# First mixer of a decoder trunk: head squares made in z's place, the inverse's transposed seed by TensorE, q halves emptied as done, scan-only products inside later merges

## What is computed

```python
c_q, c_kv, k_r, qkv, z, b_logit, a_logit = jnp.split(h @ w_in, idx, axis=-1)
q  = (rms_norm(c_q, q_norm) @ w_q_b)           # 8 heads of 96
kv = (rms_norm(c_kv, kv_norm) @ w_kv_b)        # 8 heads of 64 + 64
y_mla = causal_block_attention(rope(rms_norm(q)), rope(rms_norm(k)), v)
gq, gk, gv = jnp.split(silu(causal_short_conv(qkv, conv_w)), 3)   # 8 heads of 64 each
gq, gk = l2_norm(gq) * 64 ** -0.5, l2_norm(gk)                    # per head
# gated delta rule in 4 chunks of 64 tokens, per head:
a    = strict_lower(kb @ k.T * decay) + eye
u, w = triangular_solve(a, [vb, kb * exp(gc)])
attn = (q @ k.T) * decay;  q_dec = q * exp(gc)
for each chunk:                                 # the scan
    v_new = u - w @ state
    o     = q_dec @ state + attn @ v_new
    state = state * exp(g_last) + k_tail.T @ v_new
o = rms_norm(o, out_norm) * silu(z)
y = concat([y_mla, o]) @ w_out
```

## Time and profile before

| | |
|---|---|
| time, median of 3 | 1108.63 us (1105.33 to 1108.97) |
| profiled execution, its time | 1108.93 us |
| its span, first to last instruction | 1107.1 us |
| mean granted clock of TensorE | 0.994 |
| TensorE busy | 98% of the span |
| VectorE, ScalarE, GpSimd busy | 58%, 46%, 4% |

### The profile page before, as it was taken

The page is one execution under the profiler, slowest core; times in us unless marked ns, Lnnn a source line. Parts: engine busy times, 40 slices in busy tenths (PEclk is TensorE's granted clock), DMA queues, the critical chain, the costliest instruction groups (busy, mean ns, idle before and its releaser), DMA issues.

```text
span 1107.1 us, 18807 instructions
## 1 busy us (share of the span) xinstructions
PE 1081.3 (98%) x8329; PEld 987.0 (89%) x8329; DVE 647.3 (58%) x791; ACT 503.8 (46%) x597; POOL 47.1 (4%) x34
## 2 busy tenths in 40 slices
PE   7999999998889999999999999999999999999998
PEld 7999988987789799999889999888788889999986
DVE  5755544688665775555447555544764557555542
ACT  5644433683633354444335444434654536444430
POOL 1000000112051000000000000000100000000000
PEclk9999999999899999999999999999999999999999
DMA  9855555253002356555546565555445474665531
GB/s 311 265 181 187 189 190 178 87 190 114 1 15 68 126 184 189 188 190 191 190 152 194 188 190 191 190 185 176 153 159 218 155 228 154 192 189 190 191 114 38
DMA packets 127194, 184.91 MB, mean 167 GB/s; under 512 B 4205, under 2 KB 101722, under 8 KB 126986
## 3 DMA queue, kind: packets, MB, share of 16 engines
q1 hardware_dynamic: 126368, 181.88, 50.6%
q0 software_dynamic: 448, 1.71, 0.5%
q10 hardware_dynamic: 298, 0.12, 0.1%
HBM read 182.66 MB, written 1.05 MB: 166 GB/s over the span
## 4 chain that ended last, share of the span: by engine, by line
PE 88%; DVE 7%; ACT 2%; issue 2%; DMA 1%; POOLq 0%; SPq 0%; POOL 0%; DVEq 0%; ACTq 0%
PE B L1274 19%; PE B L1275 19%; PE B L1276 19%; PE B L1315 7%; PE B L1319 7%; PE B L1316 7%; PE B L1688 3%; DVE wlo L840 2%; DVE arena L1007 1%; PE B L1384 1%; PE B L1385 1%; PE B L1386 1%; DMA raw<-in_ffn_w_up 1%; PE B L1348 1%; PE B L1811 1%
## 5 line engine op out<-in xcount | busy, mean ns | idle before, releaser
L840 DVE TENSOR_TENSOR wlo<-raw,whi 128x2048 fp32r<-128x2048 f32 (+1 forms) x169 | 387.7, 2301 | 227.5 <-ACT whi L443 227.3
L443 ACT ACTIVATE whi<-raw 128x2048 fp32r<-128x2048 f32 (+1 forms) x171 | 324.2, 1908 | 385.2 <-PE B L1276 243.0
L1274 PE MATMUL B<-xTh,whi 128*128 128x256 f32 x1408 | 397.4, 282 | 0.3 <-DVE wlo L840 0.2
L1275 PE MATMUL B<-xTl,whi 128*128 128x256 f32 x1408 | 396.4, 282 | 0.0
L1276 PE MATMUL B<-xTh,wlo 128*128 128x256 f32 x1408 | 396.4, 282 | 0.0
L1274 PEld LDWEIGHTS B<-xTh,whi 128*128 128x128 f32 x1408 | 266.1, 189 | 1.2 <-DVE wlo L840 0.7
L1275 PEld LDWEIGHTS B<-xTl,whi 128*128 128x128 f32 x1408 | 266.3, 189 | 0.0
L1276 PEld LDWEIGHTS B<-xTh,wlo 128*128 128x128 f32 x1408 | 266.2, 189 | 0.0
L1315 PE MATMUL B<-whi,hTh 128*128 128x512 f32 x352 | 139.5, 396 | 0.0
L1316 PE MATMUL B<-wlo,hTh 128*128 128x512 f32 x352 | 139.0, 395 | 0.0
L1319 PE MATMUL B<-whi,hTl 128*128 128x512 f32 x352 | 110.6, 395 | 0.0
(11 more groups left out here) (241 smaller groups left out, 999.6 us busy)
## 6 DMA issues: line engine op xcount, KB each, us to landing
raw<-in_ffn_w_up SPq DMA_DIRECT2D x44, 1024.0 KB, 5.4
raw<-in_ffn_w_down SPq DMA_DIRECT2D x44, 1024.0 KB, 4.8
raw<-in_ffn_w_gate SPq DMA_DIRECT2D x43, 1024.0 KB, 5.5
raw<-in_sg_w_in SPq DMA_DIRECT2D x16, 1024.0 KB, 5.4
raw<-in_ab_w_in SPq DMA_DIRECT2D x8, 1024.0 KB, 5.1
raw<-in_sg_w_out SPq DMA_DIRECT2D x8, 1024.0 KB, 5.3
raw<-in_ab_w_out SPq DMA_DIRECT2D x4, 1024.0 KB, 4.8
raw<-in_ab_w_in SPq DMA_DIRECT2D x2, 832.0 KB, 4.4
```

The source lines that it names most:

```text
L443: A(whi[:, j % SLOTS, 0:kt * width], raw[:, j % SLOTS, 0:kt * width], ACT.Copy).then_inc(S("hi_ready"), 1)
L840: TT(wlo[:, j % SLOTS, 0:n], raw[:, j % SLOTS, 0:n], whi[:, j % SLOTS, 0:n].bitcast(f32), ALU.subtract).then_inc(S("lo_ready"), 1)
L1274: mm(out_ap, lh, rh, start=first, stop=False)
L1275: mm(out_ap, lh, rl, start=False, stop=False)
```

## The change

Five things, all in the first mixer. The memory places of the squares, of DT and of qd^T change with them.

1. ScalarE empties the q product's first half (t = 0) as soon as that half is done, ahead of `hi(b + 8)`; the semaphore `latent_sums` counts the first halves of q and kv.
2. VectorE makes `lo(b + 10)` right after `conv(3)` instead of after `scale_channels(4)`.
3. The head squares get one buffer, `head_squares`, where z will stand later. ScalarE squares q after `nt_out(1)`, and k after `tap(5)` once VectorE has summed q's. VectorE sums q's between `lo(b + 11)` and `conv(5)`, k's after `conv(5)`. z is copied only after both sums.
4. DT's seed is D's seed transposed by TensorE in heads 6 and 7 of the attention, through bank B3, copied by ScalarE.
5. The gram of q moves into level 2, the transpose of Am into level 3, the transposes of qd into level 4, each between a level's M1 products and its DT M1 products.

```diff
-        k_squares, q_squares = at(XT0 + 2048, 1024), at(XT0 + 3072, 1024)
+        head_squares = at(R0 + 4448, 1024)
@@ ScalarE
-            hi(b + 8)
-            act.wait_ge(S("unit_done"), B_UNIT + 1)
             for t in range(NT):
+                act.wait_ge(*((S("latent_sums"), 1) if t == 0 else (S("unit_done"), B_UNIT + 1)))
                 q0, q1 = (B[6], B[7]) if t == 0 else (B[0], B[1])
...
+                if t == 0:
+                    hi(b + 8)
...
             nt_out(1)
+            act.wait_ge(S("nt_out"), 2)
+            A(head_squares, QKVn[0].rearrange("p t n -> p (t n)"), ACT.Square).then_inc(S("head_squares"), 1)
             tap(3)
...
             tap(5)
+            act.wait_ge(S("nt_out"), 4)
+            act.wait_ge(S("head_sums"), 1)
+            A(head_squares, QKVn[1].rearrange("p t n -> p (t n)"), ACT.Square).then_inc(S("head_squares"), 1)
             for i in range(4):
                 qkT_out(i)
...
             act.wait_ge(S("unit_done"), Z_UNIT + 2)
+            act.wait_ge(S("head_sums"), 2)
             for t in range(NT):
                 A(SZ[:, t, :], B[t][:], ACT.Copy, scale=rstd[:, t:t + 1]).then_inc(S("z_out"), 1)
-            act.wait_ge(S("nt_out"), 4)
-            A(k_squares, QKVn[1].rearrange("p t n -> p (t n)"), ACT.Square).then_inc(S("head_squares"), 1)
-            A(q_squares, QKVn[0].rearrange("p t n -> p (t n)"), ACT.Square).then_inc(S("head_squares"), 1)
...
+                if h >= 6:
+                    t = h - 6
+                    act.wait_ge(S("dt_sums"), t + 1)
+                    A(DT[:, 512 * t:512 * t + 512], B[3][:], ACT.Copy).then_inc(S("dt_ready"), 1)
@@ VectorE
             conv(3)
+            lo(b + 10)
...
             scale_channels(4)
-            lo(b + 10)
             conv(4)
...
+            def head_sums(i):
+                dve.wait_ge(S("head_squares"), i + 1)
+                nc.vector.tensor_reduce(qk_head_ss[:, i, :], head_squares.rearrange("p (m d) -> p m d", d=DK),
+                                        AX.X, ALU.add).then_inc(S("head_sums"), 1)
+
             scale_channels(5)
             lo(b + 11)
+            head_sums(0)
             conv(5)
 
-            for i, a in enumerate((q_squares, k_squares)):
-                dve.wait_ge(S("head_squares"), 2 - i)
-                link(nc.vector.tensor_reduce(qk_head_ss[:, i, :], a.rearrange("p (m d) -> p m d", d=DK), AX.X, ALU.add))
+            head_sums(1)
+            dve.wait_ge(S("head_sums"), 2)
...
-            for t in range(NT):
-                dve.wait_ge(S("lt_ready"), t + 1)
-                link(TT(h3(DT, t), h3(LT, t), eight("level1"), ALU.mult))
-                TT(h3(DT, t), eight("eye64"), h3(DT, t), ALU.subtract).then_inc(S("dt_ready"), 1)
@@ TensorE
+                if h >= 6:
+                    pe.wait_ge(S("d_ready"), h - 5)
+                    if h == 6:
+                        pe.wait_ge(S("dT_out"), 4)
+                    else:
+                        pe.wait_ge(S("dt_ready"), 1)
+                    problems(h - 6, 3, D, None).then_inc(S("dt_sums"), 1)
```

More of the change, by code:

```diff
@@ L227, in build_trunk @@
         Lm, LT, AT = at(R0, 1024), at(3072, 1024), at(R0 + 5472, 1024)
-        D, DT, M1 = at(R0 + 1280, 1024), at(8192, 1024), at(2048, 1024)
+        D, DT, M1 = at(R0 + 1280, 1024), at(XT0 + 2048, 1024), at(2048, 1024)
         kbe, kt = at(9216, 1024), at(10240, 1024)
-        k_squares, q_squares = at(XT0 + 2048, 1024), at(XT0 + 3072, 1024)
-        kT, qT, qdT, wT = [at(XT0 + 1024 * i, PAIRS, SEQ) for i in range(4)]
+        head_squares = at(R0 + 4448, 1024)
+        kT, qT, qdT, wT = [at(o, PAIRS, SEQ) for o in (XT0, XT0 + 1024, 8192, XT0 + 3072)]
         qd = at(1024, NT, 512)
@@ L1125, in _ @@
                     dve.wait_ge(S("decay_exps"), 2)
[L1126 removed]
+                    link(TT(begc, beta, egc, ALU.mult))
                     dve.wait_ge(S("dec_exp"), 1)
@@ L1167, in _ @@
                        ).then_inc(S("m1_ready"), 1)
+                if n == 2:
+                    dve.wait_ge(S("dec_masked"), 1)
+                    for odd in range(2):
+                        dve.wait_ge(S("gram_sums"), odd + 3)
+                        dst, decay = decay_products(odd, Am, Dec)
+                        TT(dst, B[2 + odd][:].rearrange("p (q j) -> p q j", j=64), decay, ALU.mult
+                           ).then_inc(S("a_ready"), 1)
                 for t in range(NT):
@@ L1176, in _ @@
                     yT_lo(0, 4)
-                    dve.wait_ge(S("dec_masked"), 1)
-                    for odd in range(2):
-                        dve.wait_ge(S("gram_sums"), odd + 3)
-                        dst, decay = decay_products(odd, Am, Dec)
-                        TT(dst, B[2 + odd][:].rearrange("p (q j) -> p q j", j=64), decay, ALU.mult
-                           ).then_inc(S("a_ready"), 1)
             Y4 = Y[:, :, 512:1024].rearrange("p t (q o e) -> p t q o e", o=2, e=64)
@@ L1522, in _ @@
                                         wh[:, k, c0:c1], wl[:, k, c0:c1], k == 0, k == 1)
+                if t == 0:
+                    last.then_inc(S("latent_sums"), 1)
             last.then_inc(S("unit_done"), 1)
@@ L1533, in _ @@
                 if t == 0:
-                    last.then_inc(S("kv_sums"), 1)
+                    last.then_inc(S("latent_sums"), 1)
             last.then_inc(S("unit_done"), 1)
@@ L1636, in gram, with problems @@
                     last.then_inc(S("gram_sums"), 1)
+            def problems(t, bank, lhs, rhs):
+                for h in range(HEADS):
+                    m = slice(64 * (8 * t + h), 64 * (8 * t + h) + 64)
+                    for c in range(2):
+                        last = mm(B[bank][HC[c], 64 * h:64 * h + 64], lhs[HC[c], m],
+                                  (eye[HC[c], :] if rhs is None else rhs[HC[c], m]), start=True, stop=True)
+                return last
             head_scores(0)
@@ L1666, in _ @@
                     for t in range(NT):
-                        for i in range(HEADS):
-                            m = slice(64 * (8 * t + i), 64 * (8 * t + i) + 64)
-                            for r in HC:
-                                last = mm(B[(5, 2)[t]][r, 64 * i:64 * i + 64], Lm[r, m], eye[r, :],
-                                          start=True, stop=True)
-                        last.then_inc(S("l_sums"), 1)
+                        problems(t, (5, 2)[t], Lm, None).then_inc(S("l_sums"), 1)
+                if h >= 6:
[5 more added lines that the diff above has]
+                    problems(h - 6, 3, D, None).then_inc(S("dt_sums"), 1)
             weighted_values(HEADS - 1)
@@ L1681, in y_transposes @@
                             last.then_inc(S("yT_sums"), 1)
-            def problems(t, bank, lhs, rhs):
-                for h in range(HEADS):
-                    m = slice(64 * (8 * t + h), 64 * (8 * t + h) + 64)
-                    for c in range(2):
-                        last = mm(B[bank][HC[c], 64 * h:64 * h + 64], lhs[HC[c], m],
-                                  (eye[HC[c], :] if rhs is None else rhs[HC[c], m]), start=True, stop=True)
-                return last
             pe.wait_ge(S("pT_out"), HEADS)
@@ L1702, in _ @@
                     pe.wait_ge(S("y_mla"), 2)
-                    pe.wait_ge(S("dT_out"), 4)
+                    pe.wait_ge(S("dt_ready"), 2)
                     y_transposes(0, 4)
+                if n == 2:
+                    pe.wait_ge(S("yT_lo"), 4)
+                    gram(qT, (2, 3))
+                if n == 3:
+                    pe.wait_ge(S("a_ready"), 2)
+                    for t in range(NT):
+                        problems(t, 2 + t, Am, None).then_inc(S("a_sums"), 1)
+                if n == 4:
+                    pe.wait_ge(S("qd_ready"), 1)
+                    for i in range(2):
+                        pe.wait_ge(S("at_ready"), i + 1)
+                        for q in range(2):
+                            for t in range(NT):
+                                last = transpose(B[2 + i][:, 256 * q + P * t:256 * q + P * t + P],
+                                                 qd[:, t, P * (2 * i + q):P * (2 * i + q) + P], ident)
+                        last.then_inc(S("qdT_sums"), 1)
                 for t in range(NT):
```

19 lines of the change are left out of this document (1 added, 18 removed).

## The result

| | before | changed |
|---|---|---|
| median of 22 runs each | 1107.92 us (1105.33 to 1109.61) | 1110.39 us (1107.74 to 1114.29) |
| ratio | | 1.0032 [1.0023, 1.0041] |
| profiled execution | 1108.93 us, span 1107.1 | 1111.20 us, span 1109.4 |
| TensorE's mean granted clock | 0.994 | 0.990 |

The forecast was 1110.0. The changed kernel is 2.5 us slower. Its times don't lie around one value: 13 of the 22 are between 1107.7 and 1111.2, 9 between 1113.0 and 1114.3, and the median lies near the upper end of the lower group. The profiled execution is the slowest of the lower group.

The account below looks back on a forecast made before the run. TensorE, busy nearly all the span, was taken to bound the kernel. Terms +1.6 (to attention's end), -3.2 (to W products), +2.3 (queue) and +0.7 (scan clock) gave +1.4 us, so 1110.0 us; range 1104.5 to 1114.5.

Parts of the forecast that it names:

- Part 1: Around 238 us: TensorE's 1.64 us wait goes, VectorE gains 0.3 us; TensorE runs 2.6 us ahead, waits at 262.
- Part 2: VectorE's low part of b+11: starts 0.6 us later, bounds 0.5 earlier to 1.5 later, ends at 270.3.
- the later end: b+11's low part starts 1.5 us later; by the port rule, moving the subtraction only moves blocking to the convolution.
- Part 3: Second z product: start +5.4 us, low clock +1.9, end +7.3; with gains behind it, +1.6 at the attention's end.
- Part 4: Inverse's seed: attention ends 1.55 us later, y's transposes start -0.5; the 2.08 us wait goes, its low clock -1.6.
- Part 5: After merge 0 TensorE waits 1.0 instead of 2.12 us: -1.1; ScalarE's queue before W's copies gives back +2.3.
- The queue ahead of W's copies: ScalarE's table load, Silu and weight copies delay W's copies and the scan: +2.3 us, bounds 1.5 and 3.
- The scan's clock: Clock may fall for the scan after TensorE idles about 3.1 us: +0.7 us, bounds 0 to +4.
- terms 1 to 4: Forecast for parts 1 to 4 up to y's transposes: +1.6 us at the attention's end, then -0.5.
- R2: At 274 to 291 us the low clock persists or returns: 2.9 to 3.8 us more each, 1113 to 1117; chance 0.22.
- R1: Clock holds through the wait for squares or is back at second z product: -1.5 us, 1106.5 to 1107; chance 0.15.
- R3: ScalarE's two new waits, before second z product and W's copies, don't bite: up to -8 us, some 1102; chance 0.13.

Follow-up runs that it names:

- e8: e3 with parts 1 and 2 of the change undone: 1099.94 us, ratio 0.9924.
- e9: e3 with part 4 undone, the transposed seed made by VectorE again: 1102.62 us, ratio 0.9950.
- e3: Changed kernel with ScalarE's k square behind the four q^T/k^T copies and z's Silu plus two weight copies ahead of L^T's copies: 1099.52 us, on another chip 1100.57.
- e5: Changed kernel with part 3 undone, both squares behind z's copies in two buffers, both sums behind the last convolution: 1108.84 us, ratio 1.0015.
- e7: Changed kernel with part 5 undone, gram of q, Am's transpose and qd's transposes back at levels 0, 1 and 2: 1109.13 us, ratio 1.0013.
- e1: Changed kernel with ScalarE's square of k behind the four q^T/k^T copies instead of ahead of them: 1103.31 us, ratio 0.9957.
- e10: e9 with the next stage's two 1 MB weight loads held back until the first half of the W products is made: 1101.25 us, ratio 0.9934.

## Why the prediction was right, point by point

The time was right to 0.4 us, the sign too, and the chain of waits was the one predicted. That it was right to 0.4 us is luck, twice over. Two terms were off by over 2 us each, in opposite directions. And the forecast started from 1108.63, the median of three runs, where 22 runs gave 1107.92: a change of +1.4 was forecast, of +2.5 measured.

- **Part 1** went as described: the wait of 1.64 us is gone (the product stands at 236.31), and TensorE waits instead ahead of 263.98, 2.06 us. (The 2.6 us by which it runs ahead are not the sum of the 1.6 and 0.8 beside them; measured 2.7.) Nothing of it reaches the end: e8, with parts 1 and 2 undone, is as fast.
- **Part 2** was put 0.6 us later; the low part ends at 269.6, 0.1 sooner than before. The convolution under GpSimd's multiplies took 3.87 us after a wait of 0.98, where it took 4.21 without a wait in the trace of before, and the moved subtraction 2.28 in place of 2.82. So the move did not hand the blocking on: the later end, which went with the rule of the Trainium skill (SBUF — State Buffer, "SBUF: two separate sides"), was not reached, and the value lies between my ends, near the early one.
- **Part 3.** The chain of waits was right link by link, and two sizes were too large. Predicted for the product's start +5.4 (my lower end was 4.4), measured +4.34: the low clock was there already, but the low part landed 0.7 us earlier than in my sum, and the chain behind it was shorter. Predicted for the low clock in the product +1.9, measured 0.67 (5.01 less 4.34), since the clock came back at about 275.5. Product end +5.0, not +7.3. What it gives back was right, predicted 5.7: from the product's end to the first attention transposes it is 4.0 us less, and in the attention some 1.7. The wait ahead of the banks shrank to 1.10 us, VectorE was ready 7.5 us ahead of the first row maximum, and the attention ran at full clock. Predicted sum for y's transposes with part 4: +1.6 - 0.5 = +1.1; measured -1.03. This is the 2.1 to 2.3 us by which I overpriced the wait.
- **Part 4,** -0.5 for y's transposes: measured 0.3 by e9 against e3 and 0.4 by the two kernels with a slow attention (30.01 us from the first attention transposes to y's before, 29.58 in e5). The low clock behind it (-1.6) did go, but e7 shows that parts 4 and 5 earn it together: with one wait of about 2.1 us left, the low clock can come behind that one.
- **Part 5.** From y's transposes to the W products, predicted -1.6 - 1.1 = -2.7, measured -2.42. 0.6 us of idle marked issue is new there. The queue ahead of W's copies: predicted +2.3, measured +2.21, and TensorE's wait of 2.89 us where I had put 3.1. (The 346.8 in that working does not follow from the terms beside it: 352.8 less 3.2, 1.9, 0.9 and 0.8 is 346.0. The transposes of qd ended at about 346.6, and only two product groups of 1.0 us each, and no merge, lie between them and the W products at 348.58.)
- **The scan's clock was the step that failed in size:** +0.7 with bounds 0 and 4, measured +3.42. I took the low stretch to last as long as the short one of the earlier trace rows, 3.7 us, though the place has small matmuls with gaps, which is more like the stretch of 10.1 us in the same rows. By the windows it lasted 10.2 us here and 17.1 in the second trace. In the scan half the clock turned 8.67 us into 12.09 or 14.00.
- **The sum:** terms 1 to 4 up to y's transposes -2.1 against the forecast, the way to W +0.3, the scan +2.7. They cancel to +0.8.
- **The rivals.** R2 put a further low stretch at 274 to 291, and fell: from 276 on the clock was at 1.00 there. A long low stretch did come, at 354 to 364, but that place was a term of the forecast, with bounds to 4, and no part of R2; that the runs from 1113 to 1114.3 are in R2's bracket says nothing for its mechanism. R1 (the clock holds, or is back when the product starts) fell too: the clock was at 0.50 from 266 to about 275.5. But its price for this place came nearer than mine, as the product ended at +5.0, where R1 gives +4.4 and I gave +7.3. R3 (the queues don't bite) fell by the waits of 5.04 and 2.89 us; taking the queues away gave 1099.5 to 1100.6, near its 1102.

## What to carry to other kernels

When work is moved ahead of a wait, look at what stands behind it in the same engine's queue: here two orders on ScalarE, not the amount of work, decided between 1110 and 1100 us. Price an idle stretch of TensorE by its length plus what half the clock does to the work behind it; here the scan's chains of small dependent matmuls were slow for 3.4 to 17.1 us and lost up to 5.3, and filling the wait with idle products gave back 3.4 us of the scan (2.7 in the median). And compare one mark after another along the engine, not end times alone: e9 gave the expected time, and the expected reason was wrong.

## What the runs showed that I had not expected

- The low clock behind a wait of 2.89 to 2.90 us lasted 3.4, 10.2, 10.2 and 17.1 us in four traces (e5, the changed kernel, e1, the changed kernel again), by the granted clock of their windows; with the 3.4 us of e5 the scan took 9.84 us. One program has runs 4 us apart by this, if the reading of the two groups is right.
- A wait of 2.08 us ahead of y's transposes was followed by half the clock in the kernel before and in e10, and by full clock in e9.
- Two weight loads of 1 MB went with idle time of TensorE that no semaphore explains: 0.52 and 2.08 us marked issue while they ran or just behind them (e9), none when they were held back (e10). The kernel before has none, with the same loads; the changed one has 0.6 us.
